# Turning three of four feed-forward activation tiles with VectorE blocks and small transfers in place of TensorE transposes

## The reference, cut to what matters

```
D_MODEL, SEQ, DEPTH, D_FF = 2048, 256, 2, 4 * 2048

def squared_relu_mlp(h, w1, w2):
    z = jax.nn.relu(h @ w1)          # h: 256 x 2048, w1: 2048 x 8192
    return (z * z) @ w2              # w2: 8192 x 2048

for i in range(DEPTH):
    ...
    x = x + squared_relu_mlp(rms_norm(x, ffn_norm[i]), w_ff1[i], w_ff2[i])
```

## Time and profile before

| | |
|---|---|
| median of 3 runs | 3082.02 us (3080.9 to 3082.45) |
| the profiled execution | 3082.89 us, span 3081.1 us |
| TensorE (PE) busy | 3024.2 us, 98% of the span |
| VectorE (DVE), ScalarE (ACT) busy | 1760.4 us (57%), 1498.4 us (49%) |
| DMA, all queues | 573.80 MB, mean 186 GB/s |
| mean granted TensorE clock | 0.997 of full speed |

### The profile page before, as it was taken

The page is one execution under the profiler, slowest core; times in us unless marked ns, Lnnn a source line. Parts: engine busy times, 40 slices in busy tenths (PEclk is TensorE's granted clock), DMA queues, the critical chain, the costliest instruction groups (busy, mean ns, idle before and its releaser), DMA issues.

```text
span 3081.1 us, 37226 instructions
## 1 busy us (share of the span) xinstructions
PE 3024.2 (98%) x13900; PEld 2503.5 (81%) x13900; DVE 1760.4 (57%) x2334; ACT 1498.4 (49%) x2019; POOL 51.0 (2%) x81
## 2 busy tenths in 40 slices
PE   8999999999999999999999999999999999999998
PEld 6877888888888778778888888888888888787886
DVE  6536554545455676865554545455556557786554
ACT  6534434434344565654434444344444547786333
POOL 0000000000000000000000000000000000010000
PEclk9999999999999999999999999999999999999999
DMA  7545565565655555545565665655775555665664
GB/s 255 183 129 173 191 198 184 191 190 187 194 178 185 170 165 158 165 147 188 191 196 186 192 185 190 189 175 199 217 206 180 154 174 166 197 209 198 225 239 151
DMA packets 301161, 573.80 MB, mean 186 GB/s; under 512 B 18640, under 2 KB 43600, under 8 KB 300240
## 3 DMA queue, kind: packets, MB, share of 16 engines
q1 hardware_dynamic: 293248, 541.13, 55.8%
q0 software_dynamic: 7184, 29.63, 2.8%
q10 hardware_dynamic: 576, 0.94, 0.1%
HBM read 561.15 MB, written 10.49 MB: 186 GB/s over the span
## 4 chain that ended last, share of the span: by engine, by line
PE 85%; DVE 7%; ACT 5%; issue 2%; DMA 1%; DVEq 0%; ACTq 0%
PE acc L1683 26%; PE acc L1685 26%; PE acc L1684 26%; PE tp L1701 2%; DVE wlo L1180 2%; ACT whi L876 1%; DVE wlo L1175 1%; PE sd L1764 1%; PE sd L1746 1%; ACT prob L1093 1%; PE sd L1852 1%; ACT qk L1101 0%; ACT whi L879 0%; ACT L1093 0%; DVE set_lo L1279 0%
## 5 line engine op out<-in xcount | busy, mean ns | idle before, releaser
L1683 PE MATMUL acc<-whi,set_hi 128*128 128x512 f32 x4096 | 1620.2, 396 | 25.0 <-DVE wlo L1180 15.8
L1685 PE MATMUL acc<-whi,set_lo 128*128 128x512 f32 x4096 | 1597.3, 390 | 0.0
L1684 PE MATMUL acc<-wlo,set_hi 128*128 128x512 f32 x4096 | 1596.7, 390 | 0.0
L1180 DVE TENSOR_TENSOR wlo<-raw,whi 128x1024 fp32r<-128x1024 f32 x944 | 1130.4, 1222 | 592.6 <-ACT whi L876 591.7
L876 ACT ACTIVATE whi<-raw 128x1024 fp32r<-128x1024 f32 x944 | 969.9, 1057 | 642.1 <-PE acc L1685 611.7
L1683 PEld LDWEIGHTS acc<-whi,set_hi 128*128 128x128 f32 x4096 | 770.4, 188 | 197.7 <-DVE wlo L1180 25.8
L1685 PEld LDWEIGHTS acc<-whi,set_lo 128*128 128x128 f32 x4096 | 770.1, 188 | 162.8
L1684 PEld LDWEIGHTS acc<-wlo,set_hi 128*128 128x128 f32 x4096 | 770.8, 188 | 154.2
L1275 DVE TENSOR_TENSOR set_lo<-tp,set_hi 128x1024 fp32r<-128x1024 f32 x40 | 49.0, 1225 | 197.3 <-ACT set_hi L992 197.3
L992 ACT ACTIVATE set_hi<-tp 128x1024 fp32r<-128x1024 f32 x40 | 41.1, 1026 | 209.4 <-PE tp L1701 209.4
L1175 DVE SCALAR_TENSOR_TENSOR wlo<-raw,par,whi 128x512 fp32r<-128x512 f32 x160 | 111.9, 748 | 53.0 <-ACT whi L879 52.2
(11 more groups left out here) (229 smaller groups left out, 1167.0 us busy)
## 6 DMA issues: line engine op xcount, KB each, us to landing
raw<-in_w_ff SPq DMA_DIRECT2D x512, 512.0 KB, 4.5
raw<-in_w_in SPq DMA_DIRECT2D x248, 512.0 KB, 4.3
raw<-in_w_out SPq DMA_DIRECT2D x96, 512.0 KB, 4.4
raw<-in_w_mem_kv SPq DMA_DIRECT2D x32, 512.0 KB, 4.7
raw<-in_w_proj_a SPq DMA_DIRECT2D x32, 512.0 KB, 4.2
raw<-in_w_proj_b SPq DMA_DIRECT2D x32, 512.0 KB, 5.4
raw<-in_w_kv SPq DMA_DIRECT2D x48, 256.0 KB, 3.3
raw<-in_w_in SPq DMA_DIRECT2D x48, 256.0 KB, 3.7
```

What stands on the lines that cost most here:

```text
L1180: V.tensor_tensor(wlo[:, c], raw[:, c], whi[:, c].bitcast(f32), ALU.subtract).then_inc(w_lo, 1)
L1683: T.matmul(o, h[:, tok], whi[:, c], start=first, stop=False)
L1684: T.matmul(o, h[:, tok], wlo[:, c], start=False, stop=False)
L1685: ins = T.matmul(o, l[:, tok], whi[:, c], start=False, stop=last)
```

## The change

Of the four tails of a chunk, the first three (k < 3) take another way, and the fourth stays with TensorE. Behind slab 2 VectorE transposes `stage_b` in 32x32 blocks into the first half of `u` ("blocks"), one instruction of 128x512 for each token block, and now raises `tail_tp` itself. Behind the load of slab 6 SP waits for that and issues 16 transfers from `u` to `u`, each of 32 partitions by 1 KB (32 KB), which put each block on its right partitions in the second half of `u` ("turned"). ScalarE and VectorE then make `set_hi` and `set_lo` from `turned`, not from `tp`, behind slab 6 in place of slab 5. ScalarE's wait is for all 16 transfers (semaphore `shuffled`). Both layers and the written-out chunk do the same: 24 of the 32 tails in all, 384 transfers, 48 block transposes; 192 TensorE transposes go.

```diff
+            def shuffle(t):
+
+                sp.wait_ge(sm["tail_tp"], at(t + 1))
+                for q in range(4):
+                    for d in range(4):
+                        sp.dma_start(turned[32 * d:32 * (d + 1), 256 * q:256 * (q + 1)],
+                                     blocks[32 * q:32 * (q + 1), 256 * d:256 * (d + 1)]).then_inc(sm["shuffled"], 16)
...
                             for s in range(S):
                                 slab(cc * 8 + (g + k), s, W[w], r, col, s)
+                                if s == 6 and k < 3:
+                                    shuffle(cc * 4 + (info["tail0"] + k))
...
-                act.wait_ge(sm["tail_tp"], at(t + 1))
+                if isinstance(lent, tuple):
+                    act.wait_ge(sm["shuffled"], at((lent[1] + 1) * 256))
+                else:
+                    act.wait_ge(sm["tail_tp"], at(t + 1))
...
+                elif isinstance(lent, tuple):
+                    o = sets[dst][0][:, TOK * kt:TOK * (kt + 4)]
+                    ins = A_(o.rearrange("p (n q t) -> p n q t", q=4, t=32), tp, ACT.Copy)
...
+            def turn(t, source):
+
+                source_ready(dve, source)
+                for b in range(TB):
+                    o = blocks[:, 0:TB * GW].rearrange("p (d m b t) -> p b m d t", d=4, m=4, b=TB)[:, b]
+                    ins = V.transpose(o, stage_b[:, GW * b:GW * (b + 1)].rearrange("p (m d t) -> p m d t", m=4, d=4))
+                ins.then_inc(sm["tail_tp"], 1)
...
-                                if s == 5 and k < 4:
+                                if s == 2 and k < 3:
+                                    turn(t, ("staged", q))
+                                if s == 6 and k < 3:
+                                    tail(t, info["z"], 4 * k, None, ("turned", None))
+                                if s == 5 and k == 3:
                                     tail(t, info["z"], 4 * k, None)
...
-                                if s == 3 and k < 4:
+                                if s == 3 and k == 3:
                                     tail(cc * 4 + (info["tail0"] + k), ("staged", cc * 4 + (info["staged0"] + k)))
```

More of the change, by code:

```diff
@@ L109, in __init__ @@
         self.lent = {}
-        self.steps = {e: {} for e in ("pe", "act", "dve", "pool")}
+        self.steps = {e: {} for e in ("pe", "act", "dve", "pool", "sp")}
         self.tails = 0
+        self.turns = 0
         self.staged = 0
@@ L159, in tail, with turned @@
         self.at("dve", slab_split, "tail", t, dst, kt, gain, lent)
+        return t
+    def turned(self, slab_turn, slab_shuffle, slab_split, source, dst, kt, gain=None):
+        t, n = self.tails, self.turns
+        self.tails += 1
+        self.turns += 1
+        self.at("dve", slab_turn, "turn", t, source)
+        self.at("sp", slab_shuffle, "shuffle", t)
+        self.at("act", slab_split, "tail", t, dst, kt, gain, ("turned", n))
+        self.at("dve", slab_split, "tail", t, dst, kt, gain, ("turned", n))
         return t
@@ L282, in ffn @@
         sc.groups[first].need[S - 2] = [("tail_lo", sc.tails)]
-        sc.loops[first + 1] = dict(layer=layer, tail0=sc.tails, staged0=sc.staged, rst=rst, a=a, z=z)
+        sc.loops[first + 1] = dict(layer=layer, tail0=sc.tails, staged0=sc.staged, turn0=sc.turns, rst=rst, a=a, z=z)
         for _ in range(8 * (NCHUNK - 1)):
@@ L286, in ffn @@
         sc.tails += 4 * (NCHUNK - 1)
+        sc.turns += 3 * (NCHUNK - 1)
         sc.staged += 4 * (NCHUNK - 1)
@@ L292, in ffn @@
             sc.epilogue(g, "relu2", rst, sc.staged, sc.tails)
-            sc.tail(S * (g + 1) + 3, S * (g + 1) + 5, ("staged", sc.staged), z, 4 * i)
+            if i < 3:
+                sc.turned(S * (g + 1) + 2, S * (g + 1) + 6, S * (g + 1) + 6, ("staged", sc.staged), z, 4 * i)
+            else:
+                sc.tail(S * (g + 1) + 3, S * (g + 1) + 5, ("staged", sc.staged), z, 4 * i)
             sc.staged += 1
@@ L507, in build @@
         addend = kv[:, LB * UTW + 8 * P:LB * UTW + 8 * P + 2 * TOK]
+        blocks, turned = u[:, 0:TB * GW], u[:, TB * GW:2 * TB * GW]
         gt = x
@@ L556, in tail_bank @@
         def tail_bank(lent):
+            if isinstance(lent, tuple):
+                return turned.rearrange("p (q n t) -> p n q t", q=4, t=32)
             if lent == "sd":
@@ L580, in build @@
         out_of = [sem("group_out0"), sem("group_out1")]
-        names = ("tail_tp", "tail_hi", "tail_lo", "staged", "x_stat", "rstd_ok", "stage_th",
+        names = ("tail_tp", "tail_hi", "tail_lo", "shuffled", "staged", "x_stat", "rstd_ok", "stage_th",
                  "att_in", "att_qk", "att_score", "att_smx", "att_exp", "att_prob", "att_pt", "att_ptc",
@@ L756, in _ @@
                         slab(N(g), s, W[of.w], N(of.row), N(of.col), k, of.pieces)
+                        for _, args in sc.steps["sp"].get(S * g + s, ()):
+                            shuffle(*args)
                 else:
@@ L1154, in _ @@
                                     epi_relu2(cc * 8 + (g + k - 1), info["rst"], q, t)
-                                if s == 5 and k < 4:
+                                if s == 6 and k < 3:
+                                    tail(t, info["z"], 4 * k, None, ("turned", cc * 3 + (info["turn0"] + k)))
+                                if s == 5 and k == 3:
                                     tail(t, info["z"], 4 * k, None)
@@ L1272, in tail @@
                 h, l = sets[dst]
-                if gain is None:
+                if isinstance(lent, tuple):
+                    c = slice(TOK * kt, TOK * (kt + 4))
+                    o, i = (w[:, c].rearrange("p (n q t) -> p n q t", q=4, t=32) for w in (l, h))
+                    ins = V.tensor_tensor(o, tp, i.bitcast(f32), ALU.subtract)
+                elif gain is None:
                     c = slice(TOK * kt, TOK * (kt + 4))
@@ L1614, in _ @@
                          epi_sigm=epi_sigm, epi_proj_a=epi_proj_a, epi_proj_b=epi_proj_b, x_rstd=x_rstd,
-                         tail=tail, norm_sum=norm_sum, norm_root=norm_root, norm_scale=norm_scale,
+                         tail=tail, turn=turn, norm_sum=norm_sum, norm_root=norm_root, norm_scale=norm_scale,
                          norm_rope=norm_rope, rope_gains=rope_gains,
```

## The result

The changed kernel takes 3153.69 us (median of 4 runs, 3151.23 to 3156.36) against 3081.83 before: ratio 1.0233, interval 1.022 to 1.0246, some 72 us slower. The forecast was 3061, with a range of 3057 to 3102.

The account below looks back on a forecast made before the run. The prediction took TensorE's queue to bound the feed-forward layers. From 3082.9 us it took 21.4 for the removed transposes and added 0 for stalls: 3061.5, told as 3061 after the runs' median offset, range 3057 to 3102.

Parts of the forecast that it names:

- The gain: On TensorE, 24 of 32 tails lose their transposes, at 0.89 us each: 21.4 us, gained in full.
- VectorE's turn: Two block transposes per tail ahead of slab 3's wlo: 1.28 us the pair, 1.9 us to spare, costing nothing.
- The latest issue of slab 7's load: On SP, followed back from TensorE: issued by 349.33 at the latest, leaving the series 7.75 us.
- the gain is eaten: Rival: slab 7's load lands after 4.5 us, not 3.7 (3079), or VectorE's turn takes 2.4 us (3086); chance 0.10.
- the length of the series: SP's sixteen issues in front of slab 7's load: 0.48 us each at most, 7.6 us in all.
- no stall, price nothing: At slab 7's load on SP: the series fits its 7.75 us, so 0 us is added; chance 0.42.
- The slower case: Rival: SP's queue is full, one slow issue per series delays slab 7's load; 20 us slower, 3102; chance 0.19.
- The 50 ns and the 2 us: Skill page figures for SP's transfers: dispatch about 50 ns, sixteen issues 0.8 us; fixed part about 2 us each, 32 us unoverlapped.

Follow-up runs that it names:

- e6: As e5, with the 16 issues in four pieces of four, behind the loads of slabs 6, 7 and the next group's 0 and 1: 3057.86 us, ratio 0.9923.
- e7: As e5, with all 16 transfers of a tile issued by GpSimd in place of SP: 3057.16 us, ratio 0.9923.
- e3: The changed kernel with 8 of the 16 transfers of each turned tail left out: 3057.51 us, ratio 0.9918.
- e8: The changed kernel with its 16 transfers per tile replaced by 12 of 32 KB in four forms, from SBUF or HBM; single run: 3059.05 us.
- e4: The changed kernel with 4 of the 16 transfers of each turned tail left out: 3069.06 us, ratio 0.9954.
- e1: The changed kernel with TensorE's eight transposes per turned tail put back besides, their result not read: 3152.57 us, ratio 1.0227.
- e5: The changed kernel with set_hi and set_lo of a turned tile moved from behind slab 6 to behind the next group's slab 0: 3152.99 us, ratio 1.0228.
- e9: As e5, with the 16 issues in one piece behind the load of slab 7 in place of slab 6: 3120.9 us, ratio 1.0124.
- e10: As e5, with the 16 issues in one piece behind the next group's slab 1 load, set_hi and set_lo behind its slab 2: 3074.83 us, ratio 0.9977.

## Why the prediction was wrong

**The gain: right.** 21.4 us for 192 transposes. e6 and e7, with every transfer made, win 24 to 25 us (3057.9 and 3057.2 against 3081.9), e3 25.5 (against 3083.0). The 3 us more than the sum are explained in part. By the groups the tail costs 22.67 - 21.76 = 0.91 us, 21.8 in all. And the clock differs outside the feed-forward blocks: in the profiled execution of the kernel before it is at the lower level in three stretches ahead of the last 20 us (from 213.4, 1022.3 and 1326.1 us), in those of e6 and e7 in one; such a stretch costs some 1.5 us. e3 has three as well. Whether the kernels or the single executions make that difference stays open.

**VectorE's turn: right.** 1.30 us for the pair against 1.28, beginning 3.78 us after the group's first matmul as worked out (340.18 - 336.41 = 3.77). The first transfer went out 5.10 us after it (5.17 worked out).

**The latest issue of slab 7's load: nearly right.** It was worked out as 12.92 us after the group's start, or a series of 7.75 us. The load took 4.17 us from its issue to ScalarE, not 3.75, so the limit was 7.4: e8's series of 7.0 us and e3's of 5.2 cost nothing, e4's of 7.7, which the 7.75 would let pass, costs 12 us in all. A longer landing is what the rival "the gain is eaten" had priced, at 0.8 us; it was 0.4.

**The step that failed: the length of the series.** The prediction took "0.48 as the most it costs: 7.6 us against 7.75" and "no stall, price nothing". It measured 10.28 us, 0.64 per issue: 591 ns and a gap. I had scaled by size, on the ground that 32 KB are nearer to the smaller transfer than to a load. Every row that I used for an issue had HBM at the source; these have SBUF, and e8 shows that this makes the difference of some 160 ns. With 433 ns and the gap the series would have been about 7.6 us, as forecast, and against the limit of 7.4 still a little late. The margin of 0.15 us should have been told as no margin: the slope behind it is steep.

**A rival had the right wait, another reason and too small a price.** The slower case placed its threshold at 0.54 us per issue and the wait at slab 7. The wait was there, and 0.64 lies beyond the threshold; no run has a series near it (8.5 us). It expected one stuck issue in a series, for a full queue; in fact each was longer, for its source, so what it had of the mechanism is the late load, not the reason. At 0.64 the same formula gives 10.28 - 7.75 = 2.53 us late; the load also took 4.17 us to ScalarE in place of 3.75, so 2.95, and the series began 0.07 earlier than worked out: 2.88, as measured.

**A term that was not in the sum: the clock.** A wait of 2.9 us can be followed by matmuls at 0.43 us in place of 0.23. In the trace of the changed kernel 15 of the 24 waits are, at a granted clock of 0.50 for some 3 us each. By the spans: 72.8 = -21.4 + 66.2 (waits, 82.0 less 15.8) + 28.0. The rest of 28 us has two parts. A wait costs 0.27 us more than its idle time: the idle time is 2.72 where TensorE is 2.88 late, since the matmul ahead still counts as busy, and the matmul behind it takes 0.11 longer (to 361.40, not 361.29). That is 24 x 0.27 = 6.5 us. What is left, some 22 us, is what the lower clock makes, some 1.5 us for each of the 15. PE's busy time shows the two together: 3031.9 - 3001.8 = 30.1 us more than in e3, which has the same 13708 matmuls.

In e4, with waits of 0.9 us at most in the first loop, the clock of the run is 0.997, as before. So the loss rises steeply: 12 us at 12 transfers, 96 at 16. e1, with the transposes back, waits less (63.0 us) and loses 69.8 - 47.2 = 22.6 us besides, in place of 28.0: together 69.8 us of span against 72.8. Its first six waits, of 1.5 to 1.8 us, are followed by no fall of the clock; others, of 1.8 to 2.0 us, are. From which wait on, and why not in every group, stays open.

**A rule weighed.** The Trainium skill, in "DMA: Bandwidth & Descriptors", section "Issuing engines are not separate DMA queues", says that issuing from several engines saves only sequencer time, which is usually small. For this series it was 10 us, and e7, which against e5 does nothing but move it to another engine, turns 1.0228 into 0.9923. That only sequencer time is saved agrees with this; that it is usually small did not hold here, with 0.59 us for an issue against 1.8 from issue to landing, sixteen times in front of a load that is due. The 50 ns and the 2 us that the prediction took from the same page of the Trainium skill stand there under GpSimd's path, not SP's.

## What to carry to other kernels

A queue of issues is an engine: before putting n transfers into it, find the latest moment at which the next load behind them may go, and compare it with n times the issue's duration for that kind of source. If it does not fit, spread the issues between the loads (e6) or give them to an idle queue (e7); the transfers themselves were free here. Moving the series back in one piece still made a load late, by less (e9, e10). A margin smaller than the uncertainty of the duration, with a steep loss behind it, is a coin toss and should be forecast as one.

## What the runs showed of the hardware that I had not expected

- An issue on SP takes 584 to 601 ns for 32 KB inside SBUF, 421 to 433 ns for 32 KB from HBM, and 372 ns for a slab's 512 KB from HBM; 32 or 128 partitions make 12 to 17 ns. Of these the small transfers have the longer issues.
- The same 32 KB issue on GpSimd takes 0.49 us (7.82 us for 16), less than on SP. The transfers land 4.8 us after it (median), 1.8 after SP's in the changed kernel, 2.6 in e6.
- After 2.7 us without a matmul TensorE continued 1.3 us at full clock and then ran some 3 us at a granted clock of 0.50, in the group shown. 15 of the 24 such waits are followed by it.
- The load of slab 7 came to ScalarE 4.17 us after its issue where sixteen small transfers stood ahead of it, and 3.75 was worked out from a load with nothing right ahead.
